# Output products of blocks 1 to 3 taken block by block, a fourth weight buffer, and three unit pairs loaded ahead of the rows

## The reference, cut to what matters

```
z   = x @ W_in                       # 9 sections of 1024 columns
o_A = HGRN2 chunkwise recurrence(q, forget, i) with out-gate
o_B = B * causal_conv3(C * h)
mix = W_out( sigmoid(gate_a)*(o_A W_a) + sigmoid(gate_b)*(o_B W_b) )
x   = LayerNorm(alpha*x + mix)
x   = LayerNorm(alpha*x + PEER(x))
x   = x + sigmoid(x W_pg) * (p W_pp)

PEER, per token: 8 heads, q = x @ w_q; two score vectors of 128 per head; the top 16 of each,
  the top 16 of their 256 sums -> 16 of 16384 experts per head, g = softmax of the 16
  out = sum over 8*16 experts of  g * gelu(u_e . x) * v_e
```

## Time and profile before

| | |
|---|---|
| median of 3 runs | 1783.93 us |
| the profiled execution | 1783.08 us, its span 1781.1 us |
| PE / PEld / DVE busy | 1574.5 / 873.9 / 1315.0 us |
| ACT / POOL busy | 777.8 / 502.2 us |
| moved by DMA | 655.39 MB, of it 536.90 MB gathers |
| granted TensorE clock, mean | 0.984 |

### The profile page before, as it was taken

The page is one execution under the profiler, slowest core; times in us unless marked ns, Lnnn a source line. Parts: engine busy times, 40 slices in busy tenths (PEclk is TensorE's granted clock), DMA queues, the critical chain, the costliest instruction groups (busy, mean ns, idle before and its releaser), DMA issues. The chain is left out here.

```text
span 1781.1 us, 16905 instructions
## 1 busy us (share of the span) xinstructions
PE 1574.5 (88%) x5000; PEld 873.9 (49%) x5000; DVE 1315.0 (74%) x2711; ACT 777.8 (44%) x1937; POOL 502.2 (28%) x528
## 2 busy tenths in 40 slices
PE   8999999999999997989788668888889878787788
PEld 7888888766655575545344222332333223222224
DVE  4454588699888999678878876876666677766676
ACT  6666695422222224343334334444444443444453
POOL 0000000122222232324343443433333343333341
PEclk9999999999999999999999989999999999999999
DMA  5113289799999999999999999999999999999994
GB/s 213 66 65 141 98 323 397 285 420 420 390 420 421 421 410 405 423 415 412 421 415 422 422 422 421 421 420 422 422 421 421 421 396 423 421 421 422 421 416 183
DMA packets 94932, 655.39 MB, mean 368 GB/s; under 512 B 10368, under 2 KB 14208, under 8 KB 17152
## 3 DMA queue, kind: packets, MB, share of 16 engines
q0 software_dynamic: 73728, 536.90, 72.8%
q1 hardware_dynamic: 20832, 116.97, 16.7%
q10 hardware_dynamic: 288, 0.52, 0.1%
HBM read 652.26 MB, written 2.10 MB: 367 GB/s over the span
## 5 line engine op out<-in xcount | busy, mean ns | idle before, releaser
L2107 PE MATMUL psum<-uv,diag 128*128 128x512 f32 x1424 | 709.0, 627 | 190.6 <-ACT diag L991 187.1
L720 POOL DMA_INDIRECT uv<-in_pk_uv,idx x512 | 499.8, 976 | 1244.0 <-PE psum L2107 562.9
L1592 DVE CUSTOM_DVE_ANT_0 uv<-uv,psum 128x1024 f32<-128x1024 f32 x512 | 623.2, 1218 | 299.5 <-DMA uv<-in_pk_uv,idx 292.3
L2107 PEld LDWEIGHTS psum<-uv,diag 128*128 128x128 f32 x1424 | 257.2, 194 | 611.8 <-ACT diag L991 391.2
L979 ACT ACTIVATE gelu<-dots 128x1 f32<-128x1 f32 x512 | 103.4, 202 | 757.1 <-DVE dots L1592 755.1
L2007 PE MATMUL psum<-xT,raw 128*128 128x384 f32 x640 | 208.4, 486 | 0.0
L1605 DVE SCALAR_TENSOR_TENSOR oT<-uv,coef,oT 128x1024 f32<-128x1024 f32 x151 | 193.4, 1281 | 6.2 <-ACT coef L983 6.2
L2007 PEld LDWEIGHTS psum<-xT,raw 128*128 128x128 f32 x640 | 120.7, 190 | 81.7
L983 ACT ACTIVATE coef<-gelu,weight 128x1 f32<-128x1 f32 x512 | 150.8, 295 | 16.6
L991 ACT ACTIVATE diag<-ident,coef 128x128 f32<-128x128 f32 x356 | 143.0, 402 | 11.6
L1843 PE MATMUL psum<-xTh,w_hi 128*128 128x512 f32 x248 | 98.8, 398 | 0.1
(11 more groups left out here) (281 smaller groups left out, 1709.8 us busy)
## 6 DMA issues: line engine op xcount, KB each, us to landing
raw<-in_w_in SPq DMA_DIRECT2D x32, 1024.0 KB, 8.9
raw_a<-in_w_a SPq DMA_DIRECT2D x12, 1024.0 KB, 4.7
raw<-in_pk_w_q SPq DMA_DIRECT2D x10, 1024.0 KB, 9.3
raw_y<-in_w_in SPq DMA_DIRECT2D x8, 1024.0 KB, 6.7
raw<-in_w_branch_a SPq DMA_DIRECT2D x8, 1024.0 KB, 7.4
uv<-in_pk_uv,idx POOLq DMA_INDIRECT x512, 15.2
raw<-in_w_out SPq DMA_DIRECT2D x6, 1024.0 KB, 12.0
raw_w<-in_pk_w_q SPq DMA_DIRECT2D x6, 1024.0 KB, 10.3
```

What stands on the lines that cost most here:

```text
L720: pool.indirect_dma_start(row_uv(r)[:], None, pk_uv, bass.IndirectOffsetOnAxis(idx[:, i % 2, j:j + 1], 0)).then_inc(row_loaded(r)[0], 16)
L1592: V.tensor_tensor_reduce(u, u, x_cur[:], 1.0, 0.0, ALU.mult, ALU.add, dots[:, r % 32:r % 32 + 1]).then_inc(dot_done, 1)
L2107: last = T.matmul(B[i][:], diag[:, n % DR, :], row_uv(r)[:, D + i * 512:D + (i + 1) * 512], start=(r in FIRST), stop=last_of_block, skip_g ...
```

## The change

Five things are altered, all by tables of rows and buffers; the arithmetic is the same.
1. **Buffers.** Three more places for weights: 12 in the `scores` tensor, 13 in `gaT` and 14 in `gbT`, each in columns that are not in use yet. They hold the same [8][256] numbers, but with 512 numbers from one of the 8 to the next: 8 runs of 1 KB for each partition in place of one run of 8 KB. Pairs 2 to 10 go to 12, 13, 14, 0, 1, 2, 12, 13, 14; from pair 11 on, and for merges and outputs, the four buffers 0, 1, 2, 12 go round. A pair is loaded when the pair six earlier is done (four, from pair 15).
2. **SP.** Pairs 2, 3, 4 are issued right after query load 2, ahead of the wait for unit 1; pair 5 behind query load 5.
3. **Rows.** Units in rows 0 to 62 (before 57), merges in rows 63 to 86 (before 58 to 80), outputs in rows 88 to 99, one a row (before 83 to 93).
4. **Outputs** block by block, (b, c) with c inside; the norms from rows 95, 99, 103, the transposes at 98, 102, 106; query 0 in rows 108 to 112. The last query loads of blocks 1 to 3 are issued in the order 1, 0.
5. What follows from it: rows 0 to 102 are shared, and five of rows 109 to 121 (108 in block 0, before 102); the seventh `uv` buffer from row 98 (before 91); the search of item 8 in rows 116 to 120 with three steps a row (before 113 to 120 with two), those of items 9 and 10 in rows 123 to 134 and 137 to 148 (before 120 to 134 and 136 to 150).

```diff
@@ slot()
+            if i >= 12:
+                return (scores[:, 0, :, 2 * P:], gaT[:, :, P:P + CW], gbT[:, :, P:P + CW])[i - 12]
@@ search_rows()
             if i == PKH:
-                return [SCORE_ROW[0] + 2 + k // 2 for k in range(STEPS)]
+                return [SCORE_ROW[0] + 2 + k // 3 for k in range(STEPS)]
+            if i in (PKH + 1, PKH + 2):
+                return [SCORE_ROW[i - PKH] + 2 + k * 4 // 5 for k in range(STEPS)]
...
+        MERGE0 = 63
-        MERGE_ROW = [58 + n * 23 // 128 for n in range(16 * KT)]
-        OUT_ROW = [83 + n * 11 // 96 for n in range(4 * (TB - 1) * KT)]
-        NORM_ROW = [None] + [OUT_ROW[-1] + 1 + 2 * b for b in range(1, TB)]
+        MERGE_ROW = [MERGE0 + n * 24 // 128 for n in range(16 * KT)]
+        OUTS = [(c, b) for b in range(1, TB) for c in range(4)]
+        OUT_ROW = [MERGE_ROW[-1] + 2 + n // KT for n in range(len(OUTS) * KT)]
+        NORM_ROW = [None] + [OUT_ROW[4 * KT * b - 1] + 4 for b in range(1, TB)]
...
-        MERGE_R, QUERY_R = BLOCK_ROWS - 2 - 5 * (UV + 1), QUERY_ROW[-1][-1] + 11
+        MERGE_R, QUERY_R = BLOCK_ROWS - 2 - 4 * (UV + 1), QUERY_ROW[-1][-1] + 11
...
-        LOADS += [(("unit", n), n - 2 if n < 4 else (n - 2) % 3) for n in range(2, len(UNITS) // 2)]
-        LOADS += [(("merge", m), m % 3) for m in range(8)]
-        LOADS += [(("out", c), (c + 2) % 3) for c in range(4)]
+        RING = (0, 1, 2, 12)
+        AHEAD = (12, 13, 14)
+        LOADS += [(("unit", n), (AHEAD + RING[:3] + AHEAD)[n - 2] if n < 11 else RING[(n - 11) % 4])
+                  for n in range(2, len(UNITS) // 2)]
+        LOADS += [(("merge", m), RING[(m + 1) % 4]) for m in range(8)]
+        LOADS += [(("out", c), RING[(c + 1) % 4]) for c in range(4)]
@@ SP's program
             fetch(pk_w_q[2], "query", 0, 2)
-            sp.wait_ge(t_done, USE["unit", 1] + 1)
-            unit_fetch(2)
+            for n in range(2, 5):
+                unit_fetch(n)
             for h in (3, 4, 5):
                 sp.wait_ge(t_done, USE["query", 0, h - 3, 1] + 1)
                 fetch(pk_w_q[h], "query", 0, h)
+            sp.wait_ge(t_done, USE["unit", 1] + 1)
+            unit_fetch(5)
             sp.wait_ge(t_done, USE["unit", 3] + 1)
-            unit_fetch(3)
+            unit_fetch(6)
...
-                    sp.wait_ge(t_done, USE["unit", 2 * (n - 3) + 1] + 1)
+                    sp.wait_ge(t_done, USE["unit", 2 * (n - (6 if n < 15 else 4)) + 1] + 1)
                 unit_fetch(n)
...
             def tail_fetch(m, src, *name):
-                if m < 3:
-                    sp.wait_ge(t_done, USE["unit", len(UNITS) - 5 + 2 * m] + 1)
+                if m < 4:
+                    sp.wait_ge(t_done, USE["unit", len(UNITS) - 7 + 2 * m] + 1)
                 else:
-                    sp.wait_ge(t_done, chunk_end(m - 3))
+                    sp.wait_ge(t_done, chunk_end(m - 4))
```

More of the change, by code:

```diff
@@ L229, in build @@
         first_in = [sem(f"first_in{j}") for j in range(4)]
-        raw_in = [sem(f"raw_in{i}") for i in range(12)]
+        raw_in = [sem(f"raw_in{i}") for i in range(15)]
         consts = sem("consts")
@@ L297, in build @@
         UNIT_ROW = [[-1] * UNIT_MM] * EARLY
-        UNIT_ROW += [[(UNIT_MM * n + i) * 58 // (UNIT_MM * (len(UNITS) - EARLY)) for i in range(UNIT_MM)]
+        UNIT_ROW += [[(UNIT_MM * n + i) * MERGE0 // (UNIT_MM * (len(UNITS) - EARLY)) for i in range(UNIT_MM)]
                      for n in range(len(UNITS) - EARLY)]
@@ L301, in build @@
         UNIT_END = [rows[-1] for rows in UNIT_ROW]
-        MERGE_ROW = [58 + n * 23 // 128 for n in range(16 * KT)]
-        OUT_ROW = [83 + n * 11 // 96 for n in range(4 * (TB - 1) * KT)]
-        NORM_ROW = [None] + [OUT_ROW[-1] + 1 + 2 * b for b in range(1, TB)]
+        MERGE_ROW = [MERGE0 + n * 24 // 128 for n in range(16 * KT)]
+        OUTS = [(c, b) for b in range(1, TB) for c in range(4)]
+        OUT_ROW = [MERGE_ROW[-1] + 2 + n // KT for n in range(len(OUTS) * KT)]
+        NORM_ROW = [None] + [OUT_ROW[4 * KT * b - 1] + 4 for b in range(1, TB)]
         TURN_ROW = [None] + [NORM_ROW[b] + 3 for b in range(1, TB)]
         Q0 = TURN_ROW[-1] + 2
-        QUERY_ROW = [[Q0 + (n * 5 // 16 if h == 0 else 6 + n * 6 // 16 if h == 1 else 17 + 14 * (h - 2) + n * 9 // 16)
-                      for n in range(2 * KT)] for h in range(PKH)]
+        QUERY_ROW = [[Q0 + (n * 5 // 16 if h == 0 else 6 + n * 6 // 16 if h == 1 else 17 + n * 9 // 16)
+                      if h < 3 else 123 + 14 * (h - 2) + n * 9 // 16 for n in range(2 * KT)] for h in range(PKH)]
         SCORE_ROW = [QUERY_ROW[h][-1] + 2 for h in range(PKH)]
@@ L318, in shared @@
                     return True
-                return r % 3 == 1 and 106 <= r <= 120
+                return r % 3 == 1 and 109 <= r <= 121
             if b == 1:
@@ L475, in build @@
         rest = [("merge", 1, c, i) for c in range(4) for i in range(4)]
-        rest += [("out", 1, c, b) for c in range(4) for b in blocks(1)]
-        rest += [("turn", 1, b, kh) for b in blocks(1) for kh in range(2)]
+        for r in range(OUT_ROW[0], TURN_ROW[-1] + 1):
+            rest += [("out", 1, *OUTS[n]) for n in range(len(OUTS)) if r == OUT_ROW[KT * n + KT - 1]]
+            rest += [("turn", 1, b, kh) for b in range(1, TB) for kh in range(2) if r == TURN_ROW[b]]
         for n, name in enumerate(rest):
@@ L615, in first_parts @@
                     sp.dma_start(ln2_gain[:], ln2_g[0].partition_broadcast(P)).then_inc(ln2_in, 16)
-            for n in range(4, len(UNITS) // 2):
-                if n == 4:
+            for n in range(7, len(UNITS) // 2):
+                if n == 7:
                     sp.wait_ge(t_done, USE["query", 0, 5, 1] + 1)
-                elif n < 7:
-                    sp.wait_ge(t_done, USE["unit", 2 * (n - 3) + 1] + 1)
                 else:
-                    sp.wait_ge(t_done, USE["unit", 2 * (n - 3) + 1] + 1)
+                    sp.wait_ge(t_done, USE["unit", 2 * (n - (6 if n < 15 else 4)) + 1] + 1)
                 unit_fetch(n)
@@ L643, in query_fetch @@
                 if h < 2:
-                    sp.wait_ge(t_done, chunk_end(9 + h))
+                    sp.wait_ge(t_done, chunk_end((11, 8)[h]))
                 else:
@@ L1737, in tail_row @@
                         merge(1, n // 4, n % 4)
-                for n in range(4 * (TB - 1)):
+                for n, (c, b) in enumerate(OUTS):
                     if r == OUT_ROW[KT * n + KT - 1] + 3:
-                        residual(1, n // (TB - 1), 1 + n % (TB - 1))
+                        residual(1, c, b)
                 for b in range(1, TB):
```

6 lines of the change are left out of this document (2 added, 4 removed).

## The result

The changed kernel takes 1785.97 us (median of 12 runs), the kernel before 1782.64 in the same comparison: a ratio of 1.0019, with an interval from 1.0011 to 1.0027. By the medians that is 3.3 us slower. I had forecast 4.8 us faster. The profiled execution took 1786.75 us, its span 1784.7 (before 1781.1).

The account below looks back on a forecast made before the run. The prediction took DMA to be the full resource from about 345 us, PE and DVE close behind. Its terms -5.5 + 3.7 - 3.0 = -4.8 us took the profiled 1783.08 to 1778.3, as median 1779.1; range 1772 to 1787.

Parts of the forecast that it names:

- Loads ahead: At 326 to 340 us: four loads move in DMA's idle time before the rows, a gain of 5.5 us, bounds nothing to 8.
- part of those 4.1 us was waiting behind q1: At the first gather, 335.8:339.9: a possible earlier start of gathers, counted only in the 8 us upper bound of the gain.
- Pieces of 1 KB: Eight loads in the rows run at 356 GB/s, 0.46 us more each: +3.7 us, bounds 0 and +7.0.
- rival 1: In the rows: the 1 KB pieces cost nothing, by the skill's rule, giving 1775.4 or 1772.5 us; chance 0.17.
- The price of the taking of turns: 1 KB loads among gathers: queues alternate piece by piece, so a load takes 22.8 us instead of about 5, costing DMA nothing.
- The other estimate, under 10 us a load: 1 KB loads among gathers: by the skill's page, queues change at packets of 9 to 17 descriptors, so loads land sooner.
- rival 3: At pairs 8 to 10 and output 2: PE starves as 1 KB loads take over 24 us, 1789 us; chance 0.12.
- The wait of 8 us at the third output product: At output 2's slow load: PE waits some 8 us, of which DVE sees perhaps 2 us.
- 440:475: PE no longer behind its rows: 3.0 of 3.3 us lost come back, ACT's 5.76 us wait gone as the sign.
- Outputs, norms and six more shared rows: At 640 to 715 us: DVE gets 7.7 us more work but catches up; taken as 0, bounds -2.9 and +7.7.
- w_gate at 710.96: Behind the last norm: its load, 4 MB or 10 us of DMA, fills what DVE can't.
- Rival 2: At 640:715: DVE takes the gain through six sums and output 2, about 5 us, so 1784, no change; chance 0.19.

Follow-up runs that it names:

- after_pairs_not_ahead: The changed kernel with pairs 2, 3 and 4 issued where the kernel before issues them, not ahead of the rows: 1.0065 to the kernel before, 8.2 us slower than the changed kernel.
- ring_of_three: The changed kernel, merges taken one row after, three 8 KB buffers from pair 11, the 1 KB one only for the last output group: 1.0051 to the kernel before.
- early_outputs_61: The changed kernel with merges taken one row after, units and merges two rows earlier (61 for 63), outputs three rows earlier, block by block: 1.0042 to the kernel before.
- before_plus_ahead: The kernel before with three more buffers and pairs 2 to 4 loaded ahead, all tables of rows as before: 0.9999 to the kernel before.
- after_merge_early: The changed kernel with DVE taking each merge product one row after PE issues it, not three: 0.9997 to the kernel before, 3.9 us faster than the changed kernel.

## Why the prediction was wrong

**Loads ahead, right in kind.** 326:335 moves at 354 GB/s, as forecast. The forecast had no gathers before 340; the first came sooner after its issue than before. POOL's issue in the changed kernel, and DVE's first dot (before 346.59):

```profile
336.53 1.09 POOL L729 DMA_INDIRECT uv<-in_pk_uv,idx  x1 [333.27 <-DVE idx L1566]
...
343.25 1.22 DVE L1601 CUSTOM_DVE_ANT_0 uv<-uv,psum 128x1024 f32<-128x1024 f32 x1 [0.42 <-ACT psum L976]
```

I had left "part of those 4.1 us was waiting behind q1" as a bound only, and it was so. Issue to dot is 6.7 us here and was 10.9, and the runs test it: in all fourteen kernels with pairs 2 to 4 issued ahead it is 6.7 us, and the dot then waits for ACT; in the four that issue weights just ahead of the gather it is 10.5 to 12.3, with a wait of 4.07 to 6.04 us for the gather. `after_pairs_not_ahead` differs from the changed kernel by the moment of the loads alone. So the term is -6.7 by the rows and 8.2 us by the experiment, which also moved the 1 KB pieces, in place of -5.5.

**Pieces of 1 KB, right.** 410 and 416 GB/s against 421, +3.4 us for a forecast of +3.7; and 326:335, where the pairs move ahead of the gathers, has 354 for an estimated 356. The rule of at least 512 B for line rate (the Trainium skill, page "DMA: Bandwidth & Descriptors", section "Specifications") doesn't agree with these rows, so rival 1 fell. The price of the taking of turns was right too. From issue to landing, in 355:700 of the changed kernel (KB each, median us), the first in 8 KB pieces, the second in 1 KB pieces:

```profile
raw<-in_w_branch_a SPq DMA_DIRECT2D x2, 1024.0 KB, 15.1
scores<-in_w_branch_a SPq DMA_DIRECT2D x2, 1024.0 KB, 25.8
```

The four slow loads with no other one ahead of them (pair 18, merges 2 and 6, output 2) took 25.1 to 26.3 us, for 22.8 and a latency. Pairs 8, 9 and 10 took 31.9, 41.7 and 46.5, so the third landed 67 us after pair 8's issue, for a forecast of 68. In 380:400, while they run, q0 counts 834 packets and q1 832. The other estimate, under 10 us a load, failed. It doesn't follow from turns of several pieces either: if both queues send equally many in a turn, a load of 64 pieces still waits for 64 gather pieces. Equal counts, here and in the earlier trace rows, don't tell how many pieces a turn has; "piece by piece" was read into them.

The slow loads landed in time in the changed kernel (PE has 165.00 of 165 us in 475:640), so rival 3 didn't come, although its condition of a load over 24 us did: PE starts on the third slow pair at 458.59, 13 us after it landed. `ring_of_three` and `early_outputs_61` show how near it is. The wait of 8 us at the third output product didn't come either: PE was already 13.70 us late.

**440:475, right in size, but its sign wasn't one.** DMA is at 415 GB/s for 381. ACT's wait for PE, which I said would go, is still there: 9.0 us in all ahead of its `u_pad` rows (before 9.6), and 9.6 us in `before_plus_ahead`, where DMA is at 362. So that wait doesn't measure PE's lateness. What changed is the work that DVE gets done, 33.20 us of 35 in place of 29.75.

**Outputs, norms and six more shared rows: the step that failed.** "I take 0, bounds -2.9 and +7.7": measured +7.4, near the upper bound. Two reasons given for 0 failed. First, w_gate at 710.96 was to fill what DVE can't; it starts when the norms end, and now at 716.83, after the hole. Second, the later queries were said to "lie beside a full DMA: nothing". DMA isn't full there, because DVE holds the buffers, and those loads were what filled it: 4.14 MB in 660:700 before, 1.11 after, beside the same gathers. I counted DVE's added work and didn't ask which loads are issued while it is done. The wait itself, PE for a merge that DVE takes three rows later, I never looked for; the change that lets PE run ahead of the rows turned a harmless lag into a wait. Rival 2 had one of the two losses (the six sums, priced at half) and gave 1784, no change; it lacked PE's wait and the late loads, for which the early merges give 3.9 us.

**Still open.** 860:900 is at 384 GB/s in the changed kernel's trace and at 420 in that of `after_merge_early`, though the code in those rows is the same. One wait goes with it, DVE's for a product of block 0's last gate on PE. In the changed kernel:

```profile
865.01 0.69 DVE L1726 SCALAR_TENSOR_TENSOR gate<-gate,psum 128x512 f32<-128x512 f32 x1 [4.24 <-PE psum L2181]
```

In the ten of the eighteen traces where DVE waits 1.6 to 1.8 us in all for these products, 860:900 moves 411 to 420 GB/s; in the eight where it waits 3.0 to 4.2, 384 to 405. No edit aimed at it, so what makes PE late there isn't shown. It is 3.4 us in one execution; whether all of it is in the median isn't known, so of the 3.9 us that early merges gave back, part may lie here.

## What to carry to other kernels

Where DMA is the full resource, ask of each edit which loads are issued while another engine holds the buffers: a load that nobody waits for can still be what fills the gap. When an edit changes which engine is ahead, every fixed lag between engines has to be set again; the same two rows were worth -3.9 us in one kernel and +5 us in the other. And a gain at the start can be lost again further on: the loads ahead were worth nothing with the old rows and 8.2 us with the new ones.

## What the runs showed of the hardware

A load of 1 MB in pieces of 1 KB among gathers lands 25.1 to 26.3 us after its issue when no other such load is ahead of it, one of 8 KB pieces 15.1 (the merge weights, medians). With nothing but 1 KB pieces DMA moved 354 GB/s in 326:335, with 8 KB pieces 420 to 423. The first gather's data were used 6.7 us after its issue where the weight loads were out of the way, and 10.5 to 12.3 us after where they were issued just ahead of it.
